# Gated scan: which blocks of the level products are made, where the state update lands, when z is projected, and the order of the weight loads

## The reference, cut to what matters

```python
def step(S, blk):
    qc, vc, kc, gc = blk
    b = jnp.cumsum(gc, axis=2)
    o = jnp.einsum('bhtd,bhde->bhte', qc * jnp.exp(b), S)
    pair = jnp.exp(jnp.where(mask, b[:, :, :, None] - b[:, :, None], -jnp.inf))
    A = jnp.einsum('bhtd,bhtsd,bhsd->bhts', qc, pair, kc)
    o = o + jnp.einsum('bhts,bhse->bhte', A, vc)
    b_end = b[:, :, -1]
    S = jnp.exp(b_end)[..., None] * S + jnp.einsum('bhsd,bhse->bhde', kc * jnp.exp(b_end[:, :, None] - b), vc)
    return S, o
```

## Time and profile before

| | us |
|---|---|
| median of 3 runs (lowest, highest) | 2931.93 (2926.65, 2934.36) |
| the profiled execution | 2930.02 |
| its span | 2928.1 |
| TensorE matmul busy | 2625.7 (90%) |
| VectorE busy | 1275.8 (44%) |
| ScalarE busy | 851.3 (29%) |
| mean granted clock of TensorE | 0.941 |

### The profile page before, as it was taken

One profiled execution on the slowest core, in us unless ns is written; L12 is line 12 of the kernel. 1 busy time (PEld: TensorE's weight loads), 2 busy tenths in 40 slices (PEclk: granted clock), 3 DMA queues, 4 the chain that ended last, 5 costly groups with the idle time before them and its releaser, 6 DMA issues. The chain is left out here.

```text
span 2928.1 us, 47911 instructions
## 1 busy us (share of the span) xinstructions
PE 2625.7 (90%) x21048; PEld 1631.3 (56%) x21048; DVE 1275.8 (44%) x2035; ACT 851.3 (29%) x1562; POOL 128.0 (4%) x152
## 2 busy tenths in 40 slices
PE   7799999999899599889989889968779999989678
PEld 2454466666444288778844434424336776858533
DVE  3221344443476455445544412152514666566504
ACT  2111222234456345434412200111002334343301
POOL 0000000000022200000001000021000000000000
PEclk9799999999899799999999989969889999999789
DMA  6200111110355721133063120011022000010043
GB/s 250 81 29 6 45 49 49 49 49 35 119 149 154 177 73 54 35 116 109 18 213 130 55 81 34 0 35 44 37 76 59 22 22 8 1 44 1 15 158 100
DMA packets 102608, 203.51 MB, mean 70 GB/s; under 512 B 6527, under 2 KB 60927, under 8 KB 98816
## 3 DMA queue, kind: packets, MB, share of 16 engines
q1 hardware_dynamic: 89954, 152.61, 15.6%
q0 software_dynamic: 12448, 47.85, 5.8%
HBM read 148.01 MB, written 52.43 MB: 68 GB/s over the span
## 5 line engine op out<-in xcount | busy, mean ns | idle before, releaser
L687 PE MATMUL psum<-arena,m_fill_weight 128*128 128x512 f32 (+1 forms) x864 | 335.6, 529 | 5.9 <-DMA m_fill_weight<-in_l_w_in 5.9
L2672 PE MATMUL psum<-arena,g_weight 128*128 128x512 f32 (+1 forms) x512 | 219.7, 555 | 27.6 <-DMA g_weight<-in_l_w_in 27.6
L386 PE MATMUL psum<-arena,project_weight_y 128*128 128x512 f32 x512 | 222.8, 598 | 11.3 <-DMA project_weight_y<-in_l_w_in 11.3
L687 PEld LDWEIGHTS psum<-arena,m_fill_weight 128*128 128x128 f32 x864 | 157.2, 193 | 108.3 <-issue 91.8
L386 PEld LDWEIGHTS psum<-arena,project_weight_y 128*128 128x128 f32 x512 | 98.3, 192 | 135.5 <-issue 123.8
L386 PE MATMUL psum<-arena,project_weight_m 128*128 128x512 f32 (+3 forms) x432 | 156.8, 526 | 14.9 <-DMA project_weight_m<-in_l_w_in 14.9
L2918 DVE COPY_PREDICATED g_pairs<-g_masks,psum 128x512 f32<-128x512 uint8 x128 | 93.6, 731 | 144.4 <-PE psum L2700 144.4
L1164 PE MATMUL psum<-gp_weight,arena 128*128 128x512 f32 x320 | 147.5, 609 | 0.0
L2663 PE MATMUL psum<-g_weight,arena 128*128 128x128 f32 x1152 | 145.0, 275 | 0.0
L2061 PE MATMUL psum<-fin_weight,fin_mix 128*128 128x512 f32 x320 | 141.9, 596 | 3.1 <-POOL fin_mix L2211 3.1
L2663 PEld LDWEIGHTS psum<-g_weight,arena 128*128 128x128 f32 x1152 | 136.7, 192 | 0.0
(11 more groups left out here) (414 smaller groups left out, 4260.9 us busy)
## 6 DMA issues: line engine op xcount, KB each, us to landing
arena<-scratch_operands SPq DMA_DIRECT2D x40, 512.0 KB, 3.9
mod_weight<-in_l_mod_w SPq DMA_DIRECT2D x8, 1536.0 KB, 8.3
scratch_operands<-arena POOLq DMA_DIRECT2D x16, 640.0 KB, 8.1
scratch_operands<-arena POOLq DMA_DIRECT2D x32, 320.0 KB, 10.6
g_weight<-in_l_w_in SPq DMA_DIRECT2D x20, 512.0 KB, 4.6
m_fill_weight<-in_l_w_in SPq DMA_DIRECT2D x18, 512.0 KB, 3.8
project_weight_y<-in_l_w_in SPq DMA_DIRECT2D x4, 2048.0 KB, 7.9
scratch_spill<-m_fill_shifted POOLq DMA_DIRECT2D x12, 640.0 KB, 3.2
```

Of the source, the lines that this page charges most:

```text
L386: last = nc.tensor.matmul(p.psum[0:rows, u % 8, 0:n], lhsT, rhs, start=(k == 0), stop=(k == KT - 1))
L687: last = nc.tensor.matmul(p.psum[:, FILL + f % BANKS, 0:width], weight[:, q % PIECES, k, :], hT[:, k, at:at + width], start=(k == 0), stop ...
L2672: last = nc.tensor.matmul(bank[:, 0:width], w[:, kk, :], hT[:, kk, first:first + width], start=(kk == 0), stop=(kk == KT - 1))
```

## The change

Four things.

- `blocks(n, d)` gives, for a level, the blocks of a chunk that its mask can keep, as (key, query, size): at levels 0 to 4 and on the diagonal four blocks of 32 by 32 on the diagonal, at level 5 two of 32 by 32 beside it, at level 6 one of 64 by 64. `scores` makes these products alone, each still over all 128 rows of contraction, with `size` stationary and `size` moving columns, where there was one of 128 by 128. The rest of the bank keeps what it had, and the mask drops it.
- The update's product goes to the second quarter of the bank OUT instead of KEYS. The transpose then waits for the copy of the keys before it, no more for the state. The update waits, beside the keys' copy, for the state of the slot before and for the copies of the outputs so far, and the output products wait for the state ahead of the first of them instead of the second.
- z of a head is projected one head later: head 0's leaves slots 0 to 9, and head 3's comes into slots 80 to 87, eight of the ten of the last unit.
- SP loads the weights in the order in which `plan` uses them, and nothing else after the masks; POOL issues the four stores of `mixT`.

```diff
--- before.py
+++ after.py
@@ -2562,7 +2562,7 @@
         total = due[max(due)]
         before = total
         for name in names_of_head:
-            of = head if name != "turn" else head - 2
+            of = head - {"turn": 2, "z": 1}.get(name, 0)
             first_of[name, of] = len(fills)
             for part in parts[name]:
                 before += passes(name, part)
@@ -2573,16 +2573,18 @@
 
     LEAD = -1
     plan(("gate0", "q"), 0, LEAD, 1)
-    plan(("gate1", "v", "z"), 0, 0, SLOTS)
+    plan(("gate1", "v"), 0, 0, SLOTS)
     for head in range(1, H):
         plan(("gate0", "q", "gate1", "v", "z") + (("turn",) if head >= 2 else ()), head, SLOTS * (2 * head - 1), 2 * SLOTS)
-    for first, of in ((SLOTS * U - 3, H), (SLOTS * (U + 1), H + 1)):
+    for first, slots, name, of in ((SLOTS * U - 3, 1, "turn", H), (SLOTS * U, SLOTS - 2, "z", H), (SLOTS * (U + 1), 1, "turn", H + 1)):
         for s in range(max(due) + 1, first):
             due[s] = due[s - 1]
-        plan(("turn",), of, first, 1)
+        plan((name,), of, first, slots)
     LAST = SLOTS * (U + 1)
     ends_in = lambda f: min(s for s in due if due[s] >= fills[f][3])
-    piece_at = lambda name, head: PIECES * head + [n for n, _ in pieces].index(name)
+    column_of = dict(pieces)
+    slot_of = {name: n for n, (name, _) in enumerate(pieces)}
+    in_order = [(name, head) for name, head in first_of if name != "turn"]
 
     SCORES, KEYS, OUT, FILL = 0, 3, 4, 5
     free = arena[:, KT * TOK:]
@@ -2592,8 +2594,16 @@
     k_decayed = lambda u: free[:, at + 2 * LAT + (u % 2) * TOK:][:, 0:TOK]
     mixT = free[:, at + 2 * LAT + 2 * TOK:][:, 0:LAT]
     chunked = lambda a: a.rearrange("p (c t) -> p c t", t=C)
-    keys_bank, update_bank, out_bank = p.psum[:, KEYS, 0:P], p.psum[:, KEYS, P:2 * P], p.psum[:, OUT, 0:P]
+    keys_bank, update_bank, out_bank = p.psum[:, KEYS, 0:P], p.psum[:, OUT, P:2 * P], p.psum[:, OUT, 0:P]
     group = lambda w, n, g: 2 * (L + 1) * w + 2 * n + g
+
+    def blocks(n, d):
+
+
+        size = max(32, 1 << n) if n < L else 32
+        if n == L or 2 << n <= size:
+            return [(at, at, size) for at in range(0, C, size)]
+        return [(at + d * size, at + (1 - d) * size, size) for at in range(0, C, 2 * size)]
 
     def halves(a, n, d):
 
@@ -2622,20 +2632,18 @@
             def _(sp):
                 sp.dma_start(free[:, 0:(2 * L + 1) * P], p.dram["const_hgrn"]).then_inc(masks_loaded, 16)
                 w_view = w_dram.rearrange("(k p) n -> p k n", p=P)
+                for name, head in in_order:
+                    if head:
+                        sp.wait_ge(sig["fill_ready"], last_of[name, head - 1])
+                    col = column_of[name] + head * P
+                    sp.dma_start(weight[:, slot_of[name]], w_view[:, :, col:col + P]).then_inc(weight_loaded[slot_of[name]], 16)
+
+            @block.gpsimd
+            def _(pool):
                 for head in range(H):
-                    for name, col in pieces:
-                        n = piece_at(name, head)
-                        if n >= PIECES:
-                            sp.wait_ge(sig["fill_ready"], last_of[name, head - 1])
-                        sp.dma_start(weight[:, n % PIECES], w_view[:, :, col + head * P:col + (head + 1) * P]).then_inc(
-                            weight_loaded[n % PIECES], 16)
-                    if head >= 2:
-                        sp.wait_ge(sig["fill_copied"], last_of["turn", head - 2])
-                        sp.dma_start(mix[head - 2, :, CTX:TOK], mixT).then_inc(sig["stored"], 16)
-                for head in (H - 2, H - 1):
-                    sp.wait_ge(sig["fill_copied"], last_of["turn", head])
-                    sp.dma_start(mix[head, :, CTX:TOK], mixT).then_inc(sig["stored"], 16)
-                sp.wait_ge(sig["stored"], 16 * H)
+                    pool.wait_ge(sig["fill_copied"], last_of["turn", head])
+                    nc.gpsimd.dma_start(mix[head, :, CTX:TOK], mixT).then_inc(sig["stored"], 16)
+                pool.wait_ge(sig["stored"], 16 * H)
 
             @block.tensor
             def _(pe):
@@ -2653,10 +2661,9 @@
                             last.then_inc(sig["fill_ready"], 1)
                             yield
                             continue
-                        piece = piece_at(name, head)
-                        w = weight[:, piece % PIECES]
+                        w = weight[:, slot_of[name]]
                         if f == first_of[name, head]:
-                            pe.wait_ge(weight_loaded[piece % PIECES], 16 * (piece // PIECES + 1))
+                            pe.wait_ge(weight_loaded[slot_of[name]], 16 * (head + 1))
                         if name in ("v", "z"):
                             for t in range(*part):
                                 for kk in range(KT):
@@ -2693,12 +2700,14 @@
                         pe.wait_ge(sig["fill_copied"], last_of["q", h])
                     if m >= RING:
                         pe.wait_ge(sig["merged"], m - RING + 1)
+                    left = level(w, n) if n < L else k[:, w % 2, CTX:TOK]
+                    right = level(w, n) if n < L else q[:, h % 2, :]
                     for c in range(4 * g, 4 * g + 4):
-                        tokens = slice(c * C, (c + 1) * C)
-                        left = level(w, n)[:, tokens] if n < L else k[:, w % 2, CTX:TOK][:, tokens]
-                        right = level(w, n)[:, tokens] if n < L else q[:, h % 2, tokens]
-                        last = nc.tensor.matmul(p.psum[:, SCORES + m % RING, (c - 4 * g) * C:(c - 4 * g + 1) * C], left, right,
-                                                start=True, stop=True)
+                        for key, query, size in blocks(n, d):
+                            at = (c - 4 * g) * C + query
+                            last = nc.tensor.matmul(p.psum[key:key + size, SCORES + m % RING, at:at + size],
+                                                    left[:, c * C + key:c * C + key + size], right[:, c * C + query:c * C + query + size],
+                                                    start=True, stop=True)
                     last.then_inc(sig["scores_ready"], 1)
 
                 fill_to(due[LEAD])
@@ -2717,7 +2726,7 @@
                     part(1)
                     if scan and i < SLOTS - 1:
                         if s > SLOTS:
-                            pe.wait_ge(sig["state_ready"], (SLOTS - 1) * u + i)
+                            pe.wait_ge(sig["keys_copied"], (SLOTS - 1) * u + i)
                         nc.tensor.transpose(keys_bank, k_decayed(u)[:, c * C:(c + 1) * C], p.const("ident")).then_inc(sig["keys_turned"], 1)
                     if levels:
                         scores(w, i - 1, 0)
@@ -2726,8 +2735,8 @@
                         lat, number = c - CTX_TILES, G_LAT_CHUNKS * u + i - CTX_TILES
                         if number:
                             pe.wait_ge(sig["y_copied"], number)
+                        pe.wait_ge(sig["state_ready"], (SLOTS - 1) * u + i)
                         nc.tensor.matmul(out_bank, pairs[:, u % 2, lat, :], v[:, h % 2, c, :], start=True, stop=False)
-                        pe.wait_ge(sig["state_ready"], (SLOTS - 1) * u + i)
                         nc.tensor.matmul(out_bank, q_decayed(u)[:, lat * C:(lat + 1) * C], state[:, u % 2, :],
                                          start=False, stop=True).then_inc(sig["outputs_ready"], 1)
                     part(3)
@@ -2737,6 +2746,10 @@
                     if scan and i < SLOTS - 1:
                         number = (SLOTS - 1) * u + i
                         pe.wait_ge(sig["keys_copied"], number + 1)
+                        if number:
+                            pe.wait_ge(sig["state_ready"], number)
+                        if G_LAT_CHUNKS * u + max(i - CTX_TILES, 0):
+                            pe.wait_ge(sig["y_copied"], G_LAT_CHUNKS * u + max(i - CTX_TILES, 0))
                         nc.tensor.matmul(update_bank, keys[:, i % 2, :], v[:, h % 2, c, :], start=True, stop=True).then_inc(sig["update_ready"], 1)
                 fill_to(due[LAST])
 
```

## The result

The changed kernel takes 2841.29 us in the median (2839.57 to 2843.71), the kernel before 2932.05 us beside it: a ratio of 0.9697, 95% interval 0.9681 to 0.9713. The profiled execution took 2840.36 us, with a span of 2838.5 us. The forecast was 2848 us, its range 2824 to 2880.

What follows compares the result with a forecast made beforehand. TensorE bound the first seven stretches, it and VectorE waiting for each other once a slot. Terms -18, -57.8, -13, +5.5 and +1 sum to -82.3 us, from 2930.0 to 2848 us; own range 2828 to 2864, with rivals 2824 to 2880.

Steps and rivals of the forecast that it cites:

- Score groups: Score products on TensorE: a group falls from 0.89 to 0.55 us, 0.72 for level 6, saving 5.1 us per unit.
- narrow groups cost what 64 columns cost: Rival on score products: a group costs 0.76 us, +21 us, 2869 us in all; chance 0.16.
- The slower case: Rival: each narrow product waits for its own weight load, 0.11 us an instruction, about 3100 us; chance 0.04.
- First unit: First unit, without a scan: 59.5 to 41.5 us, -18 us, from z of head 0 leaving and cheaper scores.
- Six units: The six units after the first: -57.8 us from 410.5, by scores -30.6, idle -16, weights -6.2 and clock 5.
- the clock's 8.1: Time lost at the lower granted clock in u = 2 and u = 3: 8.1 us, 5 counted back.
- The idle allowance: TensorE's waits in the six units: 8 of 24.3 us left standing, so -16 us.
- the wait moves: Rival: VectorE stays late, now at the output products; idle and half of u = 6's gain remain, 2876 us; chance 0.12.
- Unit u = 6: Unit with no projection left, decided by VectorE's own work: 59.2 to 46 us, -13 us, between -6 and -16.
- Unit u = 7: Last unit, taking z of head 3: 20.5 us plus 5.5, slots of 2.6 us, the first about 4.2.
- the rival's +10: Rival: u = 7 stays at the lower clock, +10 us, 2858 us in all; chance 0.08.
- Stores: End of the stage: the last store, issued by POOL, takes 1 to 2 us more; counted as +1 us.

Runs made afterwards that it cites:

- e7: The changed kernel with score blocks of 64 by 64 at every level: 2865.27 us, 0.9766 of the kernel before.
- e8: The changed kernel with the same score products ordered column group by column group, so that these do not take turns: 2876.41 us.
- e4: The changed kernel with the four stores on SP again, the first ahead of head 3's weights: 2849.95 us.
- e6: The kernel before with only the update's product moved to the outputs' bank, and the waits that go with it: 2887.95 us.
- e5: The kernel before with only the narrow score blocks: 2895.34 us.
- e1: The changed kernel with the score products whole again, 128 by 128: 2872.24 us.
- e10: The changed kernel with z of head 3 in slots 70 to 76 instead of 80 to 87, and the stores on SP again: 2842.28 us.
- e12: The changed kernel with z of head 3 in slots 71 to 76 instead of 80 to 87, and the stores on SP again: 2835.97 us.
- e3: The changed kernel with z projected with its own head again: 2844.85 us.

## Why the prediction was right

The place, the direction and the terms hold; the sum was 6.7 us too high. Point by point:

- **Score groups.** 0.58 us against 0.55, 0.80 for level 6 against 0.72: 14 x 0.31 + 2 x 0.09 = 4.5 us a unit in place of 5.1. The nearest rows with 64 columns gave the structure: in e7 the 64-column group costs 0.81. The rival "narrow groups cost what 64 columns cost" would have needed that in the changed kernel; e7 shows it was worth 20.0 us, against the 21 put down for it. The slower case (a product waiting for its own weight load, 0.11 us) is refuted by 12 ns an instruction (0.39 / 32); its sum was off too, since 2930 + 256 - 46 is 3140 and not about 3100 us. The Trainium skill's rule that the prediction weighed (TensorE: Matmul & The Clock Gate, Part 3), by which weight loads overlap running matmuls only between groups of rows, doesn't fit this trace: all these products use all rows, and what e8 loses, 0.45 us a group, is the turns of the column groups.
- **First unit.** 42.1 us, 41.5 forecast. It is still TensorE's: busy 41.48.
- **Six units.** -63.2 us, -57.8 forecast. Scores 6 x 4.5 = 27.0 (30.6); idle 24.3 to 5.25, so 19 (16); weights 6.2 (6.2), shown by e4; the clock's 8.1 in full (5), since the mean is 1.00. The rest, 3 us, I did not take apart. The idle allowance and the clock were both sized too low. A part of the 8 us of idle left over rested on a misread row: the longest wait of 5.0 us in the earlier trace rows lies in u = 6, and in the six units none was over 2.1. The rival "the wait moves" holds only in a small part: the output products wait 2.5 us there.
- **Unit u = 6.** 45.0 us, 46 forecast; e6, with 13.0 us of the 13.8, shows that it is the transpose's wait in the main; the narrow products alone take off 3.9 (e5), and 0.7 once the wait is gone (e1).
- **Unit u = 7.** 23.9 us, 26 forecast: the slot is 2.57 us as worked out, but the first takes 3.6, not 4.2, and the second, with no output product in it, 2.1. The clock is up from the second slot on, so neither the 0.5 for its rise nor the rival's +10 came. The low start does cost: 1.5 us against the 22.5 of e1, e4, e7 and e8.
- **Stores.** POOL costs 1.0 us at the end, as forecast (e10 and e12: 16.6; e1 to e3 with POOL: 17.6).

Undone one at a time, the four edits are worth 29.7 + 45.4 + 6.9 + 6.7 = 88.7 us of the stage's 90.0; 1.5 us of clock in u = 7 are taken off the first and the last of these. The largest part is not the narrow products but the bank.

## What to carry to other kernels

When two engines wait for each other once a step, look for the wait that a shared buffer causes and not the data: here moving one product to another bank was worth 45.4 us, more than the 29.7 of making the score products narrow, and the waits it added at the update cost nothing (TensorE never stopped there for the state or for the outputs), as the work ahead had waited for the same thing. Price a new instruction shape by the nearest shape in the trace, split into changes of shape at the ends and the rhythm within one part of the array; here their sum carried over to within 0.03 us a group (0.08 for level 6). Free time on an engine is not free at every point of a step: z's passes fitted into unit u = 6 by their sum, and the unit still became 3.7 us longer.

## What the hardware showed that was not expected

- Products with all 128 rows and 32 stationary columns run side by side on four column groups: 12 ns an instruction against 26 with the same products in another order, and 0.61 us for eight instructions that all lie in one column group of 64.
- A part of the price of a change of shape stands in the neighbours' rows: four instructions of a projection take 1.91 us between narrow score groups and 1.72 between whole ones.
- In u = 7 the granted clock is 0.93 with z in its slots and 0.63 without (e3): there z's work, 14.3 us in the earlier trace rows's rhythm, cost 5.6 us of time.
